# Norms of a four-layer transformer kernel: the last residual tile finished ahead, shifts applied later, and the sums of squares added up on VectorE

## The reference

```
def rms_norm(x, g, eps):                    # first block
    return x * rsqrt(mean(x * x, -1) + eps) * g
def _layer_norm(x, g, b):                   # second block
    mu = x.mean(-1); var = square(x - mu).mean(-1)
    return (x - mu) * rsqrt(var + 1e-5) * g + b

for layer in range(2):                      # first block
    x = x + mixer(rms_norm(x, ...)); x = x + conv_ffn(rms_norm(x, ffn_norm[layer]))
x = rms_norm(x, final_norm)
for l in range(2):                          # second block
    x = _layer_norm(ALPHA * x + (gate_a * y_ret + gate_b * y_ml) @ w_out[l], ln1_g[l], ln1_b[l])
    x = _layer_norm(ALPHA * x + (silu(gate) * up) @ w_down[l], ln2_g[l], ln2_b[l])
```

## Time and profile before

| | us |
|---|---|
| median of 3 runs | 3188.18 |
| the runs | 3188.18, 3188.3, 3179.6 |
| the profiled execution | 3181.84 |
| its span on the core | 3180.0 |
| PE busy in it | 3115.1 |
| DVE busy | 1572.7 |
| ACT busy | 1117.8 |
| POOL busy | 48.5 |

### The profile page before, as it was taken

The page is one execution under the profiler, slowest core; times in us unless marked ns, Lnnn a source line. Parts: engine busy times, 40 slices in busy tenths (PEclk is TensorE's granted clock), DMA queues, the critical chain, the costliest instruction groups (busy, mean ns, idle before and its releaser), DMA issues.

```text
span 3180.0 us, 35087 instructions
## 1 busy us (share of the span) xinstructions
PE 3115.1 (98%) x13959; PEld 2504.3 (79%) x13964; DVE 1572.7 (49%) x2324; ACT 1117.8 (35%) x1728; POOL 48.5 (2%) x45
## 2 busy tenths in 40 slices
PE   8989999999999999999999999999999999999998
PEld 6748888887688888777888878887777888878886
DVE  5574675356557652554524463334654424453324
ACT  3354443223644432334423243222334323342222
POOL 1001000100010000000000000000000000000000
PEclk9999999999999999999999999999999999999999
DMA  5302323343022223412232322323312232223321
GB/s 183 118 8 82 104 93 99 99 135 100 2 92 93 97 95 100 139 46 87 67 99 87 99 83 97 98 95 106 113 47 80 76 97 93 90 89 95 98 93 67
DMA packets 86338, 289.30 MB, mean 91 GB/s; under 512 B 11304, under 2 KB 11320, under 8 KB 85920
## 3 DMA queue, kind: packets, MB, share of 16 engines
q1 hardware_dynamic: 83584, 278.96, 27.8%
q0 software_dynamic: 1440, 6.00, 0.5%
q10 hardware_dynamic: 1152, 2.10, 0.2%
HBM read 272.33 MB, written 2.10 MB: 86 GB/s over the span
## 4 chain that ended last, share of the span: by engine, by line
PE 91%; DVE 4%; ACT 2%; issue 1%; DMA 0%; POOL 0%; ACTq 0%; DVEq 0%; POOLq 0%
PE banks L377 74%; PE banks L439 8%; PE banks L704 2%; PE banks L406 1%; PE banks L512 1%; PE banks L683 1%; PE banks L481 1%; DVE x_resid L1557 1%; PE banks L536 1%; PE banks L524 1%; DVE x_resid L1543 0%; ACT x_resid L1025 0%; PE banks L461 0%; PE banks L731 0%; PE banks L757 0%
## 5 line engine op out<-in xcount | busy, mean ns | idle before, releaser
L1202 DVE TENSOR_TENSOR w_lo<-w_raw,w_hi 128x1024 fp32r<-128x1024 f32 (+1 forms) x512 | 614.9, 1211 | 953.6 <-ACT w_hi L797 952.4
L797 ACT ACTIVATE w_hi<-w_raw 128x1024 fp32r<-128x1024 f32 (+1 forms) x512 | 527.0, 1041 | 877.7 <-PE banks L377 795.2
L377 PE MATMUL banks<-h_hi,w_hi 128*128 128x512 f32 x2304 | 713.5, 391 | 10.4 <-DVE h_lo L1281 10.4
L377 PE MATMUL banks<-h_lo,w_hi 128*128 128x512 f32 x2304 | 710.9, 390 | 0.0
L377 PE MATMUL banks<-h_hi,w_lo 128*128 128x512 f32 x2304 | 710.6, 390 | 0.0
L377 PEld LDWEIGHTS banks<-h_hi,w_hi 128*128 128x128 f32 x2304 | 432.1, 188 | 100.3 <-issue 12.0
L377 PEld LDWEIGHTS banks<-h_lo,w_hi 128*128 128x128 f32 x2304 | 433.4, 188 | 90.4
L377 PEld LDWEIGHTS banks<-h_hi,w_lo 128*128 128x128 f32 x2304 | 433.4, 188 | 90.4
L377 PE MATMUL banks<-hid_hi,w_hi 128*128 128x512 f32 x692 | 213.8, 390 | 0.0
L377 PE MATMUL banks<-hid_hi,w_lo 128*128 128x512 f32 x692 | 213.1, 389 | 0.0
L377 PE MATMUL banks<-hid_lo,w_hi 128*128 128x512 f32 x692 | 213.0, 389 | 0.0
(11 more groups left out here) (273 smaller groups left out, 3162.9 us busy)
## 6 DMA issues: line engine op xcount, KB each, us to landing
w_raw<-weights SPq DMA_DIRECT2D x496, 512.0 KB, 3.6
scratch<-scratch SPq DMA_DIRECT2D x128, 64.0 KB, 2.0
w_raw<-weights SPq DMA_DIRECT2D x16, 256.0 KB, 2.6
scratch<-scratch SPq DMA_DIRECT2D x32, 128.0 KB, 2.4
x_resid<-x_fm ACTq DMA_DIRECT2D x8, 256.0 KB, 10.5
decay<-tables POOLq DMA_DIRECT2D x2, 1024.0 KB, 6.7
y_fm<-x_resid SPq DMA_DIRECT2D x8, 256.0 KB, 2.0
rope<-tables POOLq DMA_DIRECT2D x2, 512.0 KB, 4.8
```

The source lines that it names most:

```text
L377: mm = e.matmul(bank[b][:, :], wt[:, k, j * P:(j + 1) * P], a[:, kt, :], start=kt == 0 and step == 0, stop=kt == k_tiles - 1 and step == 2)
L797: e.activation(m.w_hi[u % HL][:, 0:n], m.raw[u % RAW][:, 0:n], ACT.Copy).then_inc(*mark("w_hi", u))
L1202: e.tensor_tensor(m.w_lo[u % HL][:, 0:n], m.raw[u % RAW][:, 0:n], f32(m.w_hi[u % HL][:, 0:n]), ALU.subtract).then_inc(*mark("w_lo", u))
```

## The change

The following is changed.

1. Before r0, r1 and r2 the last two units (4 + 2 k tiles) are done tile by tile: 18 matmuls for tile 6, then 18 for tile 7 (`tile_by_tile`). Before u0 and u1 it stays at 12 + 12.
2. Before r0, u0, r1 and u1 the split of the unit that `next_unit` would make in the last panel's last unit is held back (`hold_last`): ACT makes its `w_hi` behind the root of the norm, DVE its `w_lo` behind the first `h_lo`.
3. In the layer norms the squares of tiles 4 and 5 are made and added in the first unit of the last panel, no longer behind that panel's splits.
4. The shifts of x come late: ACT makes them two tiles at a time, between the panels of the following products (`shifts`).
5. In the norms f0, d, f1 and r0 DVE adds up the squares that POOL added before (`tally_square`), and in f0, d and f1 it adds those of tiles 6 and 7 as well, so that PE makes one set of sums (`flush_tally`) where it made three. The norm e is as before.
6. In the last norm, r2, PE spreads the mean and the inverse root a second time into banks 0 and 1, ACT copies both to SBUF, and POOL normalises tiles 6 and 7 (two additions, two multiplications); DVE does tiles 0 to 5, ACT adds all shifts, for tiles 6 and 7 together with the gain (`last_tiles`).

```
@@ pe_program
-                if split_end and panel == tiles // 2 - 1 and kt + nk == k_tiles:
-                    for j, b in enumerate(banks):
...
+                if split_end and panel == tiles // 2 - 1 and k_tiles - kt <= 6:
+                    tile_by_tile(st, f0, banks, kt, k_tiles, hi, lo, u)
                     break
+    def flush_tally(st):
+        w.wait_ge(*after("sq_tally", (st, 7)))
+        sum_square(m.tally, True, True, (st, 7))
+        freed[SUMSQ] = ("root", st)
...
-                    beside=lambda: flush_squares(st), after_panel=lambda: spread_for_products(st))
+                    beside=lambda: flush_tally(st), after_panel=lambda: spread_for_products(st))
...
+        else:
+            for b, row in ((0, 212), (1, 208)):
+                bank_is_free(b)
+                spread_columns(b, row).then_inc(*mark("row_again", (st, b)))
@@ act_program, layer_norm
         e.activation(stats[:, 208:212], stats[:, 220:224], ACT.Sqrt, bias=m.eps[:, 1:2]).then_inc(*mark("root", st))
+        next_unit()
         if split:
             for f in range(DT):
                 w.wait_ge(*after("x_normed", (st, f)))
                 e.activation(m.h_hi[:, f, :], m.x[:, f, :], ACT.Identity, bias=m.p(shift, f)).then_inc(*mark("h_hi", (st, f)))
+        return shifts(st, shift)
+    def shifts(st, shift):
+        yield
         for f in range(DT):
...
+            if f % 2:
+                yield
+    def last_tiles(st, gain, shift):
+        for b, row in ((0, m.r_bc), (1, scr[3])):
+            w.wait_ge(*after("row_again", (st, b)))
+            e.activation(row[:, :], bank[b][:, :], ACT.Copy).then_inc(*mark("row_copy", (st, b)))
+        for f in range(DT):
+            w.wait_ge(*after("x_normed" if f < ON_POOL else "scaled_pool", (st, f)))
+            e.activation(m.x[:, f, :], m.x[:, f, :], ACT.Identity, bias=m.p(shift, f),
+                         scale=1.0 if f < ON_POOL else m.p(gain, f)).then_inc(*mark("x_shifted", (st, f)))
@@ dve_program
+    def tally_square(st, f):
+        w.wait_ge(*after("squared", (st, f)))
+        if f > 1:
+            w.wait_ge(*after("sq_tally", (st, f - 1)))
+        e.tensor_tensor(m.tally[:, :], m.tally[:, :], scr[4 + f % 2][:, :], ALU.add).then_inc(*mark("sq_tally", (st, f)))
...
-        for tiles in walk.fm(DT, k_tiles, in_third=centre):
-            if tiles[0][0] == 6:
-                add_square(4, 4)
-                add_square(5, 5)
+        for tiles in walk.fm(DT, k_tiles, within={2: centre, 3: squares_four_five}, hold_last=True):
@@ pool_program
-        tally_squares(f"f{n}")
-        tally_squares("r0" if n else "d")
...
+    for f in range(ON_POOL, DT):
+        e.tensor_tensor(m.x[:, f, :], m.x[:, f, :], m.r_bc[:, :], ALU.add).then_inc(*mark("recentred_pool", (last, f)))
```

More of the change, by code:

```diff
@@ L275, in __init__, with fm @@
         self.next_unit, self.turn = next_unit, 0
-    def fm(self, tiles, k_tiles, tile0=0, beside=None, in_third=None):
+    def fm(self, tiles, k_tiles, tile0=0, beside=None, within={}, hold_last=False):
+        units = -(-k_tiles // 4)
         for panel in range(tiles // 2):
-            for _ in range(-(-k_tiles // 4)):
-                self.next_unit()
+            for n in range(units):
+                if not (hold_last and panel == tiles // 2 - 1 and n == units - 1):
+                    self.next_unit()
                 if beside:
@@ L348, in unit_is_split, with tile_by_tile @@
         return u
+    def tile_by_tile(st, f0, banks, kt0, k_tiles, hi, lo, u):
+        units, kt = [], kt0
+        while kt < k_tiles:
+            if units:
+                u = unit_is_split()
+            units.append((u, kt, UNITS[u][3]))
+            kt += UNITS[u][3]
+        for j, b in enumerate(banks):
+            for u, kt, nk in units:
+                wh, wl = (t[u % HL][:, 0:nk * 256].rearrange("p (k c) -> p k c", k=nk) for t in (m.w_hi, m.w_lo))
+                for k in range(nk):
+                    for step, (wt, a) in enumerate(((wh, hi), (wh, lo), (wl, hi))):
+                        mm = e.matmul(bank[b][:, :], wt[:, k, j * P:(j + 1) * P], a[:, kt + k, :],
+                                      start=False, stop=kt + k == k_tiles - 1 and step == 2)
+                if j:
+                    mm.then_inc(*mark("gemm", ("unit", u), *[("tile", st, f0 + 1)] * (kt + nk == k_tiles)))
+            if not j:
+                mm.then_inc(*mark("gemm", ("tile", st, f0)))
     def gemm_fm(st, tiles, k_tiles, hi, lo, ready, evacuated, tile0=0, beside=None, after_panel=None,
@@ L608, in ffn @@
             gemm_fm("g" + tag, 2, DT, m.h_hi, m.h_lo, ready, lambda f: ("gate_in" if conv else "gate_act", (tag, f)), 2 * panel,
-                    beside=(lambda: flush_squares(st)) if first else None,
+                    beside=(lambda: flush_tally(st)) if first else None,
                     after_panel=(lambda: spread_for_products(st)) if first else None)
@@ L811, in square @@
         if f >= 3:
-            w.wait_ge(*after("tally", (st, f - 2)))
+            w.wait_ge(*after("tally" if st == "e" else "sq_tally", (st, f - 2)))
         e.activation(scr[4 + f % 2][:, :], m.x[:, f, :], ACT.Square).then_inc(*mark("squared", (st, f)))
@@ L827, in residual @@
     def residual(gemm, st, k_tiles, gain, beside=None):
-        for tiles in walk.fm(DT, k_tiles, beside=beside):
+        for tiles in walk.fm(DT, k_tiles, beside=beside, hold_last=not gain):
             if not gain and tiles[0][0] == DT - 2:
@@ L980, in conv_ffn, with ffn @@
                 hidden(tag, tiles, "hid")
-    def ffn(tag):
+    def ffn(tag, beside):
         for panel in range(FT // 2):
+            next(beside, None)
             for tiles in walk.fm(2, DT, 2 * panel):
@@ L1128, in act_program @@
                 e.activation(scr[f % 2][:, :], bank[b][:, :], ACT.Copy).then_inc(*mark("rope_copy", (L, f)))
+            next(shifting, None)
+        for _ in shifting:
+            pass
         for panel in walk.tm(iter(())):
@@ L1229, in residual @@
                     low_part(st, f, gain)
+            for f, _ in tiles:
+                if f and (st != "r0" or f < 6):
+                    tally_square(st, f)
     def centred_residual(gemm, st, k_tiles):
@@ L1553, in layer_norm @@
         w.wait_ge(*after("spread", st))
-        for f in range(DT + 1):
+        for f in range(DT + 1 if split else ON_POOL):
+            if f == 2:
+                next_unit()
             if f < DT:
@@ L1558, in layer_norm @@
                                        ALU.mult, ALU.mult).then_inc(*mark("x_normed", (st, f)))
-            if f < 6:
+            if f < (6 if split else ON_POOL - 2):
                 recentre(f + 2)
@@ L1826, in pool_program @@
         e.dma_start(m.select, table(tables, "select")[0:NH2, :]).then_inc(*mark("tables_in", "select" + L, by=16))
+    last = f"r{DEPTH}"
+    w.wait_ge(*after("row_copy", (last, 0)))
+    for f in range(ON_POOL, DT):
+        e.tensor_tensor(m.x[:, f, :], m.x[:, f, :], m.r_bc[:, :], ALU.add).then_inc(*mark("recentred_pool", (last, f)))
+    w.wait_ge(*after("row_copy", (last, 1)))
+    for f in range(ON_POOL, DT):
+        w.wait_ge(*after("recentred_pool", (last, f)))
+        e.tensor_tensor(m.x[:, f, :], m.x[:, f, :], scr[3][:, :], ALU.mult).then_inc(*mark("scaled_pool", (last, f)))
 def sp_program(e, fl, m, weights, y_out):
```

46 lines of the change are left out of this document (23 added, 23 removed).

## The result

The changed kernel takes 3160.1 us in the median (3159.1 to 3161.1, 4 runs), the kernel before 3188.2 (3179.6 to 3188.8, 4 runs beside them). The ratio is 0.9918, with a 95% interval of 0.9901 to 0.9935. The forecast was 3165 us, and faster; 3160.1 lies in its range, 4.9 us under it. The profiled execution took 3160.78 us against 3181.84, which is 21.1 us less where the sum said 19.2.

A forecast was written before the change was run, and what follows sets the result against it. PE's chain (91% of the span) was taken as the bound. Terms summed to 19.2 us, giving 3162.6 from the profiled execution or 3169.0 from the median; the forecast was 3165 us, range 3156 to 3177.

The forecast's parts named there:

- One set of sums: In f0, d and f1 PE loses eight small matmuls each, 1.79 us per norm, 5.37 us in all.
- C: Rival: in f0, d, f1 DVE's additions fall behind a `w_lo`, PE waits; 3.6 us less gain, 3168; chance 0.05.
- r0: In norm r0 DVE is no longer late to tile 7; all of the 1.60 us is gained.
- u0: In norm u0: 0.28 us from DVE freed, less 0.37 stall from the held split, plus 1.46 from late shifts.
- The late shifts: Behind u0, r1 and u1 PE's wait for the fourth weight unit's `w_lo` goes: 1.46 us each.
- r1: In norm r1: x addition 2.99 us earlier, clock stays up 3.49, less 0.37 stall, plus 1.46 from late shifts.
- B: Rival: the clock falls in the norms whatever the wait; 8.7 us gained, 3175; chance 0.09.
- r2: In the last norm: tile 7's x addition 0.67 us earlier, last shift 1.2 us earlier with POOL free.
- the one named as its weakness: In r2, whether POOL runs free beside DVE: 1.2 us gained, or 2.9 us lost if it cannot.
- A: Rival: POOL is held up in r2; loss of 4.1 us against the sum, 3169; chance 0.12.
- D: Rival: the held split starves the weight ring behind r0, u0, r1, u1; about 4 us slower, 3188; chance 0.04.
- E: Rival: terms right, but the runs' slow level prevails or widens, hiding part of the gain; 3172 to 3180; chance 0.08.

The follow-up runs named there:

- the filled one: Kernel before with 13 more unused matmuls in r1 between the last residual matmul and the sums of x: 3185.1 us, ratio 0.9999.

## Why the prediction was right, step by step

Where the 21.0 us of the profiled spans went, from the same instructions in both traces:

| | sum | measured | how read |
|---|---|---|---|
| f0, d, f1 | 5.37 | 5.37 | product behind the sums, 3 x (2.60 - 0.81) |
| ahead of r0, not counted | 0 | 1.36 | 1276.89 - 1270.16, less 5.37 |
| r0 and up to u0 | 1.60 | 1.59 | 564.68 for 566.27 between the last residual matmuls of r0 and u0 |
| u0 and up to r1 | 1.37 | 1.65 | 369.11 for 370.76, read likewise |
| r1 and up to u1 | 7.57 | 8.02 | 567.53 for 575.55 |
| u1 and up to r2 | 1.37 | 2.29 | 369.12 for 371.41 |
| r2 | 1.87 | 0.80 | 16.40 - 15.60 |

*One set of sums* was right to the hundredth, with the slack that was named (0.96 us for 0.8), so C is out. *r0* was right. *u0* was right but for a small part. The stall at the second low part was put at 0.37 us; it is 0.31, and taking it away gave 0.33. The late shifts gave more than their 1.46 us: from the first low part to the fourth unit are 16.34 us (1860.56 - 1844.22) for 17.62, which is 1.28 less though 0.31 of stall came in, so 1.6. The idle time of 1.46 is counted from the end of a matmul of 0.39 us, but the next could start 0.227 us after its start, so 0.16 has to be added to a wait. That counts in u0, r1 and u1.

*r1* was right in both halves. The wait for the sums is 0.20 us and the four sums take 1.05. In all ten traces of kernels that keep the 18 + 18 matmuls and the held split, r1 took 9.38 or 9.39 us and r0 6.85 to 6.88. With longer waits it was 10.91 (a wait of 0.82 us), 13.85 (3.11) and, in the kernel before, 15.83 (3.15). That is the evidence that the clock's part belongs to the late x addition. Its size does not: 3.49 us is what one trace of before happened to show. B was wrong for r0 and r1 and half right for u1, where the clock fell in five of the same ten traces and took 0.6 to 1.1 us; in u0 it fell in one, for 1.5 us. PE's wait for the sums was 0.2 us in all of them, so a short wait does not by itself keep the clock up. In the two traces compared it fell in u1 only before the change, and that is 0.68 of the 0.9 us by which this term was too small.

*r2* is the term that was mis-sized, for another reason than the one named as its weakness. POOL ran free, so A is out, and with the clock up the new r2 takes 14.67 us, 1.73 less than before for the 1.87 of the sum. The step that failed is that the clock was not reckoned with here: its fall in the profiled execution cost 0.93 of them.

The 1.36 us ahead of r0 were not in the sum. Most of them (1.26 by f0) are in and around norm e, which the change leaves alone. There the clock was low from 26.5 to 36.7 before and from 28.9 to 35.8 after. They are no gain of the change: the two traces of the changed kernel come to r0's last residual matmul at 1270.16 and 1266.78, 3.4 us apart with no edit. So the nearness of 21.1 to 19.2 is in part luck. D did not come: no wait for a weight unit is in the list.

*The median.* The sum was laid between two levels of before's runs, and they are no levels. In 29 runs beside the experiments before took 3179.6 to 3189.9 us, with a mean granted clock of 0.991 in the runs from 3179.6 to 3184.8, 0.990 from 3184.4 to 3187.3, and 0.988 or 0.989 from 3185.6 to 3189.9. 0.003 of 3180 us are 9.5 us, about the whole spread. The changed kernel ran at 0.993 to 0.995. That the clock falls in other norms of before too is shown by the second trace of its stream, the filled one: r0 took 11.13 us there and u0 11.18, where the first trace had 8.40 and 9.63. So the change takes away more than its sum says, 25 us from before's usual run. The likely reason, argued and not shown by an experiment, is that it takes away waits behind which the clock sometimes falls. E expected that the higher of the two levels would hide part of the gain; the opposite came. Why one execution falls in r0 and another does not is open.

## What to carry to other kernels

Count a wait of TensorE in front of small matmuls twice: once as time, and once as a risk of the clock, which costs 0.9 to 3.5 us per norm here when it comes (the length of r0 or r1 above the undisturbed one, less the wait) and goes with the spread of the runs. When an operation is moved out of an engine's way, look at what its place was holding up and at what it holds up now: without the held split the larger tile-by-tile part loses more than it gains (3170.9 us against 3163.0 with the smaller part and the split held), and with it the late shifts are worth 6.1 us instead of 4.4. Before GpSimd is set beside VectorE, look at where VectorE's operands lie; one of them in PSUM made the difference between 14.7 and 19.0 us.

## What was not expected of the hardware

VectorE beside GpSimd, both with two operands in SBUF: up to 1.75 us for a 128x512 operation that takes 0.68 or 0.74, and 1.7 for GpSimd's 1.25. The clock of TensorE fell in u1 in five of ten traces and stayed up in five, with the same instructions and a wait of 0.2 us in each. Twelve unused matmuls, about 2.7 us of PE's time in two waits of the first attention, took away 10.2 us at the lower clock and 3.9 us of the median.
